# Product-key gates with both 16-bit parts in one product per token

## What is computed

```python
s = jnp.einsum('thcd,ckd->thck', q, subkeys)          # 8 heads, 2 x 128 sub-keys
sv, si = lax.top_k(s, PEER_TOPK)
cand = sv[:, :, 0, :, None] + sv[:, :, 1, None, :]
cv, ci = lax.top_k(cand, PEER_TOPK)                   # 16 experts per head and token
experts = (ea * PEER_KEYS + eb).reshape(T, 128)       # 128 of 16,384 experts per token
gate = jax.nn.softmax(cv, axis=-1).reshape(T, 128)
act = jax.nn.gelu(jnp.einsum('cd,ced->ce', xc, u_tab[ec]))
y = jnp.einsum('ce,ced->cd', act * gc, v_tab[ec])
```

## Time and profile before

| | |
|---|---|
| median of 3 runs | 3779.86 us (3778.77 to 3782.63) |
| the profiled execution's own time | 3779.92 us |
| span of its instructions | 3778.1 us |
| TensorE busy | 3637.9 us, 96% |
| VectorE busy | 1917.7 us, 51% |
| ScalarE busy | 1146.6 us, 30% |
| GpSimd busy | 360.3 us, 10% |
| first PEER layer, from the first piece to the last down | 353 to about 1040 us |
| second PEER layer, the same | 1388 to about 2089 us |

### The profile page before, as it was taken

One profiled execution on the slowest core, in us unless ns is written; L12 is line 12 of the kernel. 1 busy time (PEld: TensorE's weight loads), 2 busy tenths in 40 slices (PEclk: granted clock), 3 DMA queues, 4 the chain that ended last, 5 costly groups with the idle time before them and its releaser, 6 DMA issues.

```text
span 3778.1 us, 55586 instructions
## 1 busy us (share of the span) xinstructions
PE 3637.9 (96%) x23568; PEld 2589.5 (69%) x23568; DVE 1917.7 (51%) x3415; ACT 1146.6 (30%) x1733; POOL 360.3 (10%) x213
## 2 busy tenths in 40 slices
PE   8999999999999999999999999999899999999997
PEld 7799888888887998888987865767633333333333
DVE  4588576768664885767696333556421111111111
ACT  3243344444532433444445212333210000000011
POOL 0044300000000432000000000212000000000000
PEclk9899999999998999999999999999899999999999
DMA  5544344445446444444454312211489999999996
GB/s 200 211 174 163 135 168 177 160 177 181 169 153 227 164 163 139 158 178 178 175 172 171 133 66 100 90 67 64 163 371 421 427 428 427 427 428 427 428 427 271
DMA packets 81024, 846.24 MB, mean 224 GB/s; under 512 B 8896, under 2 KB 11072, under 8 KB 12512
## 3 DMA queue, kind: packets, MB, share of 16 engines
q1 hardware_dynamic: 80768, 842.60, 56.8%
HBM read 841.52 MB, written 1.05 MB: 223 GB/s over the span
## 4 chain that ended last, share of the span: by engine, by line
PE 83%; DMA 10%; DVE 4%; ACT 2%; issue 1%; POOL 0%; DVEq 0%; ACTq 0%; SPq 0%
PE bank L88 81%; DMA ring<-in_w_gu_dram 10%; ACT arena L114 1%; PE bank L101 1%; DVE arena L124 1%; DVE arena L138 1%; DVE arena L168 0%; DVE arena L156 0%; DVE arena L132 0%; DMA ring<-in_w_inA_dram 0%; ACT L114 0%; DVE arena L144 0%; DVE ring_rounded L124 0%; POOL ring_rounded L124 0%; DVE arena L130 0%
## 5 line engine op out<-in xcount | busy, mean ns | idle before, releaser
L88 PE MATMUL bank<-arena 128*128 128x32 f16 (+7 forms) x8020 | 922.2, 328 | 37.0 <-DVE arena L124 11.9
L88 PEld LDWEIGHTS bank<-arena 128*128 128x128 f16 (+4 forms) x8020 | 502.4, 132 | 451.3 <-issue 335.7
L124 DVE TENSOR_TENSOR arena<-arena 128x512 f16<-128x512 f16 (+6 forms) x768 | 531.9, 719 | 55.8 <-ACT arena L114 40.4
L114 ACT ACTIVATE arena<-bank 128x256 f32<-128x256 f32 (+2 forms) x443 | 203.0, 458 | 1164.3 <-PE bank L88 940.2
L88 PE MATMUL bank<-ring,arena 128*64 128x512 f32 (+1 forms) x1968 | 502.8, 596 | 39.7 <-DMA ring<-in_w_gu_dram 36.2
L88 PE MATMUL bank<-xhi,ring_rounded 128*128 128x256 f32 x1744 | 489.2, 280 | 0.0
L88 PE MATMUL bank<-xhi,uhi 128*128 128x256 f32 x1552 | 453.0, 292 | 6.5 <-DVE ring_rounded L124 5.8
L88 PE MATMUL bank<-xlo,uhi 128*128 128x256 f32 x1552 | 437.1, 282 | 0.0
L88 PEld LDWEIGHTS bank<-ring,arena 128*64 128x64 f32 (+1 forms) x1968 | 170.3, 144 | 361.2 <-issue 281.9
L88 PE MATMUL bank<-vhi,phi 128*128 128x512 f32 x1024 | 408.0, 398 | 2.0 <-DVE ring_rounded L124 2.0
L88 PE MATMUL bank<-vhi,plo 128*128 128x512 f32 x1024 | 403.5, 394 | 0.0
(11 more groups left out here) (144 smaller groups left out, 3216.9 us busy)
## 6 DMA issues: line engine op xcount, KB each, us to landing
ring<-in_w_gu_dram SPq DMA_DIRECT2D x97, 2048.0 KB, 23.8
ring<-in_peer_u_dram SPq DMA_DIRECT2D x128, 1024.0 KB, 6.7
ring<-in_peer_v_dram SPq DMA_DIRECT2D x128, 1024.0 KB, 5.1
arena<-in_w_dn_dram SPq DMA_DIRECT2D x62, 2048.0 KB, 22.4
arena<-in_w_gu_dram SPq DMA_DIRECT2D x43, 2048.0 KB, 22.3
ring<-in_w_hg_dram SPq DMA_DIRECT2D x14, 2048.0 KB, 8.4
ring<-in_w_mod_dram SPq DMA_DIRECT2D x12, 2048.0 KB, 7.8
ring<-in_w_inA_dram SPq DMA_DIRECT2D x8, 2048.0 KB, 7.8
```

Source lines behind the costliest of these rows:

```text
L88: i = self.e.matmul(o, l, r, start=start, stop=stop)
L114: self.e.activation(o, i, f, scale=scale, **kw).then_inc(self.sem, 1)
L124: self.e.tensor_tensor(o, a, b, op).then_inc(self.sem, 1)
```

## The change

Both parts of a gate now stand side by side: `Boh` is laid out token, part, key, so that one matmul of 64 columns per token computes the products with the high and with the low part next to each other. A piece then has 16 matmuls and weight loads in place of 32, and 16 x 64 = 1024 columns, which fill both banks of `bG`. The two parts are added by VectorE: two `tensor_reduce` (one for each bank, 512 elements in and 256 out) write a new tile `gsum` in SBUF, and the `scalar_tensor_tensor` that multiplies `H` reads `gsum` in place of the bank. Since a piece fills both banks, `pe_build(n)` waits for the reductions of piece `n - 1` ("parts joined"), where it waited for the gate of piece `n - 2`. The new instructions settle: the first reduction and the multiplication wait until all earlier VectorE instructions are done.

```diff
-        Boh = [ar(512).bitcast(F16).rearrange("p (k t b) -> p k t b", k=2, t=16) for _ in range(2)]
+        Boh = [ar(512).bitcast(F16).rearrange("p (t k b) -> p t k b", t=16, k=2) for _ in range(2)]
         eqb = [ar(256).bitcast(F16).rearrange("p (t b) -> p t b", t=16) for _ in range(2)]
+        gsum = ar(512).rearrange("p (b t) -> p b t", t=16)
@@ pe_build
-            P.wait_ge(*(at["gated", l, n - 2] if n >= 2 else at["experts", l]))
+            P.wait_ge(*(at["parts joined", l, n - 1] if n >= 1 else at["experts", l]))
             P.wait_ge(*at["keys hot", l, n])
             P.wait_ge(*at["gates hot", l, n])
             for i in range(16):
-                P.mm(bG[n % 2][:, i * 32:i * 32 + 32], [(ah[:, i, :], bh[:, k, i, :]) for k in range(2)])
+                P.mm(bG[i // 8][:, i % 8 * 64:i % 8 * 64 + 64], [(ah[:, i, :], bh[:, i, :, :].rearrange("p k b -> p (k b)"))])
@@ dve_gates_hot
             for k in range(2):
-                V.tt(pairs(Boh[n % 2][:, k, :, :]), pairs(eqb[n % 2]), bc(gsb[:, k, t0:t0 + 16, :], 2, 16), MUL, lag=k)
+                V.tt(pairs(Boh[n % 2][:, :, k, :]), pairs(eqb[n % 2]), bc(gsb[:, k, t0:t0 + 16, :], 2, 16), MUL, lag=k)
@@ dve_gate
-            g = bG[n % 2][:, :].rearrange("p (t b) -> p b t", t=16)
+            for j in range(2):
+                V.red(gsum[:, :, 8 * j:8 * j + 8], bG[j][:, :].rearrange("p (t k b) -> p b t k", t=8, k=2), ADD, lag=j)
+            V.mark("parts joined", l, n)
...
-                V.stt(h, g[:, b0:b0 + k, :], 1.0 / LIFT, h, MUL, MUL, lag=FREE)
+                V.stt(h, gsum[:, b0:b0 + k, :], 1.0 / LIFT, h, MUL, MUL, lag=0 if b0 == 0 else 1)
```

## The result

The changed kernel takes 3817.39 us in the median of 4 runs (3812.72 to 3825.65), the kernel before 3779.32 us: a ratio of 1.0096, with a 95% interval of 1.0084 to 1.0107. That is slower by 38 us; the forecast was 28, with a range of 3785 to 3850. The profiled execution took 3815.56 us, 35.6 more than that of before.

The account below looks back on a forecast made before the run. TensorE bounds the kernel, with VectorE becoming the bound in pieces 48 to 63. Per layer -5.1 + 7.7 + 11.6 = +14.2 us, for two layers +28.4: 3779.9 + 28.4 = 3808 us, range 3785 to 3850.

Parts of the forecast that it names:

- What TensorE saves: TensorE's build of each piece: 16 matmuls at 30 ns save 0.34 us, bounds 0.18 and 0.41.
- What VectorE pays: VectorE from gate to gate: two reductions and settling add 1.45 us per piece, bounds 1.22 and 2.0.
- both bounds for dearer instructions: VectorE, per piece: 16-bit products losing their speed would cost 0.69 us for 0.42, raising the extra to 2.0.
- the formula 31e - 32s - 19.85: Sum per layer in us, e VectorE's extra and s TensorE's saving per piece; zero at e = 0.99 for s = 0.34.
- Pieces 0 to 15: VectorE's 1.99 us wait absorbs its extra work; TensorE gains 0.34 us on 15 pieces, -5.1 us per layer.
- the new wait is free here: Builds 0 to 15: reductions of the previous piece end about 7 us, or 3.4, before the build, costing nothing.
- Pieces 16 to 47: Longer gate delays odd builds' hot matrices: stall 1.16 us against 0.68 saved, net +0.48 per pair, +7.7 us per layer.
- Pieces 48 to 63: VectorE becomes the bound, 7.27 us between builds instead of 6.49, +0.78 for 14 intervals; +11.6 us per layer.
- The first interval: Build 48 to build 49: hot matrices have 0.54 us of slack, so the interval grows by 1.06 us.
- VectorE hides its part: Rival, all pieces: 63 of 64 builds per layer save 0.34 us, 3737 us; this side's chance 0.10.
- Dearer instructions: Rival on VectorE: lost 16-bit speed or slower strided reductions make the extra 2.0 us per piece, 3849 us; chance 0.17.
- that rival: TensorE's clock falls in the new 1.2 us gaps and stays low for pieces 48 to 63, +180 us, 3988; chance 0.02.

Follow-up runs that it names:

- without the addition: Changed kernel with the two reductions gone, the gate read from the banks in two multiplications, low 16-bit part left out: 3740.10 us against 3780.71, ratio 0.9885.
- pieces 0 to 15 alone: Pieces 0 to 15 in the new form, 16 to 63 in the form of the kernel before: 3769.64 us against 3781.33, ratio 0.9978.
- pieces 16 to 47 alone: Pieces 16 to 47 in the new form, the rest as in the kernel before: 3802.29 us, ratio 1.0055.
- earlier hot matrices alone: Kernel before with only the hot matrices of pieces 16 to 47 one main-loop step earlier: 3778.65 us against 3780.71, ratio 0.9994.
- VectorE's work alone: Kernel before plus two unused reductions ahead of each gate and a settling gate, still 32 matmuls and double banks: 3841.08 us against 3780.71, ratio 1.0165.
- pieces 48 to 63 alone: Pieces 48 to 63 in the new form, the rest as in the kernel before: 3813.03 us, ratio 1.0078.
- the wait alone: Kernel before with each build waiting for the gate of the piece just before it: 3781.13 us against 3781.33, ratio 1.0000.
- pieces 0 to 47, earlier: Pieces 0 to 47 in the new form, 48 to 63 old, hot matrices of 16 to 47 one step earlier: 3750.16 us against 3780.71, ratio 0.9913.
- all pieces, earlier: Changed kernel with hot matrices of all pieces from 16 on one main-loop step earlier: 3776.73 us against 3782.00 for the kernel before, ratio 0.9981.

## Why the prediction was right

Step by step, as it put them.

*What TensorE saves.* I took 30 ns for a matmul of 64 columns and a saving of 0.34 us per piece. The new builds take 0.64 us with 16 matmuls of 0.193 us each, so they start (0.64 - 0.19) / 15 = 30 ns apart, and the kernel without the addition shows 0.36 us per piece in its periods. Right. Matmul by matmul the starts are 29 to 30 ns apart. The Trainium skill, "TensorE: Matmul & The Clock Gate", section "Back-to-back issue gap", has one price of about 25 ns for 1 to 64 columns; the trace disagrees at 64, and its measurement decides. The Trainium skill, "VectorE: DVE Perf Modes", section "The TRN2 errata", gives max(60, 6 + columns) cycles, by estimate 29 ns for 64 columns at 2.4 GHz, and the trace agrees.

*What VectorE pays.* Forecast 1.45 us per piece. The two reductions are 0.69 us each, the 16-bit products kept their 0.42, so both bounds for dearer instructions fell. From the start of the split at 869.29 to the hot matrices at 872.55 it is 3.26 us; before, the same two instructions took 1.14 + 0.61 = 1.75. So e = 1.51. The term that I had too small is the settling: the first reduction starts 0.11 after the split has ended (869.29 + 1.22 = 870.51 to 870.62), where I had taken 0.03 from three short instructions. With e = 1.51 and s = 0.35 the formula 31e - 32s - 19.85 gives 15.8 us per layer; the stretches show 16.1 and 15.1.

*Pieces 0 to 15.* Forecast -5.1, measured -4.8 and -6.2, and -4.9 and -4.6 when alone; up to the first down it is -4.8 in all four. Right in the sum. The last build's saving is taken back by a longer wait for GpSimd's split, as forecast (the 0.23 us at 446.84). That the new wait is free here was wrong at one build: before build 8 it costs 0.24 us, which is nearly all of the 0.3 that are missing.

*Pieces 16 to 47.* Forecast a stall of 1.16 before odd builds only, +7.7 per layer. The stall is 1.24, only there, of which 0.06 is the larger e, and the sum is +8.6 and +8.9. The experiments with the earlier hot matrices show that this order was the cause.

*Pieces 48 to 63.* Forecast VectorE without a gap, 7.27 us between builds, +11.6. Measured 7.33 and +12.3. The 14 intervals make 14 x 0.84 = 11.7 of it. Two small terms were wrong and nearly cancel. The first interval was to grow by 1.06 and grew by 9.90 - 9.32 = 0.58: VectorE's gate of piece 48, which waits 3.40 us for ScalarE, starts 4.00 us after the build's start where it was 4.35, so it moved forward with the shorter build, and the prediction let TensorE alone come sooner. (With the long builds and the reductions, the interval is 10.24.) And the last build was to give back 0.34 and gives nothing, since the down behind it waits for a split by VectorE. The shift in order changed nothing in the distance of the builds, the reductions alone produced it, and so it is load.

*The rivals.* That VectorE hides its part fell, though its time is real once the addition is left out (3740). Dearer instructions fell with the rows of 0.69 and 0.42. The clock stayed at 1.00 in every stretch with the 1.07 us gaps. The price of that rival, 3988, was too high by itself: its 5.6 us for each two steps are counted from the old distance of 6.49, and the 28.4 that lead to the new one are added again.

*What the sum left out.* 28.4 was forecast; 35.6 was measured in the profiled executions. Of the difference 2.8 lie in the stretches with pieces (31.2 less 28.4), mostly the settling. The other 4.4 lie where the change touches nothing, above all in the second layer's mixing stage. These windows cover it in the kernel before and in the changed one, with columns as in the earlier trace rows:

```profile
1103.00:1180.00 77.00, 71.32 (x783) 63.80 (x780) 50.95 (x88) 37.24 (x73) 0.00 (x0) 0.91 0.52 194
1180.00:1220.00 40.00, 38.23 (x175) 21.53 (x173) 20.09 (x38) 3.23 (x8) 0.00 (x0) 0.91 0.39 142
```

```profile
1120.00:1200.00 80.00, 74.30 (x765) 66.10 (x762) 49.91 (x86) 36.48 (x72) 0.00 (x0) 0.85 0.47 171
1200.00:1240.00 40.00, 39.15 (x183) 22.03 (x184) 19.13 (x38) 2.30 (x8) 0.00 (x0) 0.91 0.43 164
```

A mean granted clock of 0.91 over 77 us means 0.18 x 77 = 14 us at the lower of the two levels, 1.2 GHz; 0.85 over 80 us means 24. Ten more microseconds at half speed can cost up to 5, by this estimate. The same stretch between the layers' pieces is longer by 5.0 us in the kernel with pieces 0 to 15 alone and 7.2 in the one without the addition, both faster kernels, and 0.7 shorter in the one with the reductions alone. So it isn't tied to the change's sign. It does follow the clock. In the 78 us that end 207 us ahead of build 0 of the second layer, the same instructions in every kernel, the mean granted clock and the growth of the stretch between the layers are:

| kernel | clock | growth, us |
|---|---|---|
| before | 0.91 | 0 |
| pieces 16 to 47 alone | 0.91 | 0.0 |
| earlier hot matrices alone | 0.91 | 0.0 |
| VectorE's work alone | 0.91 | -0.7 |
| pieces 48 to 63 alone | 0.89 | 1.7 |
| the wait alone | 0.89 | 1.6 |
| pieces 0 to 47, earlier | 0.89 | 1.6 |
| pieces 0 to 15 alone | 0.87 | 5.0 |
| changed | 0.85 | 6.0 |
| all pieces, earlier | 0.85 | 8.0 |
| without the addition | 0.82 | 7.2 |

Why the clock falls longer in one execution of that stage than in another was not settled. Outside the pieces the executions differ by several microseconds either way, so how near a total comes to its forecast is partly luck; the forecast is borne out by the stretches, +16.1 and +15.1 us for the 14.2 of the sum.

## What to carry to other kernels

An engine that is busy half of the time overall can still be the bound in the stretch where the work is added: read the slack at the instruction that is due next (here 0.78 and 0.59 us), not the share of the span. Before work is moved to another engine, write down what stands behind it in that engine's list and when each of these is due; where order is the cause, moving the producer one step earlier gave the gain back, and where load is the cause, it gave back one microsecond in twelve, and keeping the old form was what helped. Whether a cheaper addition would fit was not tried; by the prediction's formula it would have to cost VectorE less than 0.99 us per piece. A change that trades one engine for another can be worth taking in the stretches that have room and not in the others: here that was 30.5 us faster than before, in place of 38 slower.

## What the runs showed of the hardware

The multiplication that now reads two SBUF operands is held up by GpSimd's split in the stretch of pieces 0 to 15, and the split is no longer held up by VectorE. VectorE, then GpSimd, in the changed kernel, against the earlier trace rows:

```profile
359.90 1.29 DVE L150 TENSOR_REDUCE arena<-bank 128x256 f32<-128x512 f32 x2 [0.63 <-PE bank L88]
361.23 2.62 DVE L138 SCALAR_TENSOR_TENSOR arena<-arena 128x512 f32<-128x512 f32 x1
363.77 2.34 DVE L124 TENSOR_TENSOR arena<-arena 128x2048 f16<-128x2048 f16 x4
...
360.96 2.35 POOL L124 TENSOR_TENSOR ring_rounded<-ring,uhi 128x1024 fp32r<-128x1024 f32 x1 [4.50 <-ACT uhi L114]
```

The multiplication lasts 2.62 us in place of 0.69 and ends at 363.85, 0.54 after GpSimd's instruction at 363.31. The four 16-bit instructions are back at 2.34 from 4.52, and GpSimd's at 2.35 from 3.24. Whichever comes second waits for the whole of the other: in the kernel before, GpSimd came 0.20 us behind VectorE's comparison of 1.22 and lasted 0.89 longer, and then VectorE's next instruction lasted 2.59 and ended 0.28 after GpSimd's. The Trainium skill, "SBUF — State Buffer", section "SBUF: two separate sides", describes this as an exclusive lock on a shared port pair, taken by a VectorE instruction with two SBUF inputs against one of GpSimd that reads SBUF; the trace agrees. An instruction with one input in PSUM isn't held up here: in the kernel with VectorE's work alone, 18 multiplications that read a bank and SBUF overlap a split of GpSimd's and each last 0.69, while in the changed kernel the 12 that overlap one last 1.33 to 2.63; reductions that read a bank stay at 0.68 to 0.69 in both.

Settling doesn't cost the same everywhere: 0.11 us from the end of a 1.22 us split to the start of the reduction, 0.03 from the end of the second reduction (870.62 + 1.29 = 871.91) to the multiplication at 871.94. The first of them waits for the build's semaphore too; whether that makes the difference was not tried.
